# A decoder trunk with gated experts: router and gathered rows made from the unnormalised residual, and expert weights loaded in runs of four rows

## The chip, the cores and the metric

The kernel runs on one core of a Trainium2 chip. The time is the device time of one execution in microseconds (us); the median of three runs of the kernel before is 721.51 us (719.81 to 723.47).

## The reference

256 tokens of 1024 channels (float32) pass two layers. Each adds a mixer's output to the residual `h`, then that of a mixture of experts (MoE). The first mixer is an RWKV-7 recurrence, the second a stick-breaking attention. The MoE, where the change is made:

```python
def rmsnorm(x, g):
    return x * rsqrt(mean(x * x, -1) + 1e-6) * g

h = h + hier_moe(rmsnorm(h, norm_ffn[l]), ...)

def hier_moe(x, w_group, b_group, w_inner, b_inner, w_gate, w_up, w_down):
    pg = softmax(x @ w_group + b_group)          # 4 groups; the best one is taken
    pi = softmax(inner logits of that group)     # 4 experts of it; the best two are taken
    gates = p_group * renormalised top-2 weights # (tokens, 16 experts)
    h = silu(x @ w_gate[e]) * (x @ w_up[e]) * gates[:, e]    # 1024 -> 256
    return sum over e of h @ w_down[e]                       # 256 -> 1024
```

At the end the residual is normalised once more. Since the root factor of the norm is one number for a token, `x @ w` equals that number times `(h * g) @ w`.

## The kernel before

Phases run one after another: `rwkv`, `moe0`, `attn`, `moe1`. Each engine's program is written out by hand in the order in which it issues, and semaphores join them (`wait_ge`, `then_inc`); an engine that waits holds up all that stands behind it in its own program. The residual `h` lies token-major (two tiles `j` of 128 tokens by 1024 channels); a half `a` is 512 of the channels. The last projection of a mixer adds half 0 to `h` (DVE, L1164), and one weight piece (5.5 us) later half 1.

**Head of a MoE phase.** ACT squares `h` with a running sum (L702); DVE makes mean, reciprocal (L1136, L1137), ACT the root `rstd` (L706); DVE writes the normalised rows `xs` (L1171). TensorE waits with filler products of the identity matrix (`stay_warm`, L1738), turns `xs` into channel-major `xT` (L1747), ACT and DVE copy it from PSUM (L733, L1176); TensorE forms the logits in two steps (L2208, L2213) with ACT's copy `lgT` (L737) between. DVE adds the bias (`lg`, L1183), ranks (L1187 to L1192), marks `chosen` (L1218); TensorE counts places (L2221); DVE builds a 0/1 matrix `pick` (L1262) for each pair of experts with 64 slots for each expert. Meanwhile `xs` is split in two parts of lower precision whose sum is exact enough: `xt_hi` by ACT (L728), `xt_lo` by GpSimd (POOL, L672). TensorE gathers rows by a product of `pick` with both (L2244) and turns them (L2288), and the experts begin.

**Experts.** Eight pairs. For each: gate and up products in one row of PSUM, two experts side by side in column halves of the array (L2299), silu on ACT (L786), gate factor on DVE (L1289), down product (L2313), scattering back (L2329) and addition to `h` (L1303). 24 loads of 2 MB (two experts, half of gate and up, or the down weights) come through SyncE's queue in a ring of seven buffers (`load_bufs`, L458, L464); the two rings of the mixers' weights (`w_ring`) are two of them. In `moe0` the first two pieces of the attention's weights are split into high and low parts (ACT L691, DVE L1126) ahead of the last pair's silu in ACT's and DVE's programs.

## Time and profile before

| | |
|---|---|
| profiled execution, its span | 724.1 us, 721.9 us |
| granted TensorE clock, mean | 0.974 |
| TensorE busy (products) | 658.4 us, 91% |
| DVE / ACT / POOL busy | 354.8 / 272.5 / 101.7 us |
| read from memory | 143.11 MB |
| DMA packets under 2 KB, of all | 70449 of 97732 |

The page gives busy time for each engine, the span in 40 slices, the chain of work that ended last and the costliest groups. A timeline row names start, length, engine, line, what is written from what, and in brackets how long the engine stood idle before and what released it. The MoE phases cover about 275 to 424 and 563 to 714 us.

### The profile page before, as it was taken

How to read it: one execution, taken by the hardware profiler on the slowest of the kernel's cores; microseconds unless marked ns; L12 is line 12 of the kernel's file. 1: busy time of each engine (PE TensorE's matmuls, PEld its weight loads, DVE VectorE, ACT ScalarE, POOL GpSimd, SP SyncE). 2: the span in 40 equal slices, each digit the busy share in tenths (PEclk: the TensorE clock that was granted, in tenths of full speed). 3: DMA queues.
4: the chain of work that ended last, by engine and by line, in shares of the span. 5: the costliest groups of instructions: out<-in, count | busy, mean ns of one | idle time of the engine just before them, and what ended most of it. 6: DMA issues, size and time to landing. Idle time of an engine off the chain costs nothing. (4 is left out here: it accounts for less than half of the span.)

```text
span 721.9 us, 14225 instructions
## 1 busy us (share of the span) xinstructions
PE 658.4 (91%) x6183; PEld 455.1 (63%) x6183; DVE 354.8 (49%) x541; ACT 272.5 (38%) x387; POOL 101.7 (14%) x126
## 2 busy tenths in 40 slices
PE   2699989988988799999999999999979999999994
PEld 1575857868778578644444369997757864444442
DVE  3893896733565664312222455577734431222225
ACT  3454552442252513432222345566632342222213
POOL 9820054040032012000000000022210200000000
PEclk9799989999999999999999999999989999999999
DMA  9950532300000169999999821553104999999941
GB/s 260 301 188 14 182 131 111 96 4 5 4 4 5 60 208 364 369 365 367 366 366 377 301 94 60 175 156 136 60 0 132 357 366 367 367 367 368 367 165 60
DMA packets 97732, 145.15 MB, mean 201 GB/s; under 512 B 4745, under 2 KB 70449, under 8 KB 97665
## 3 DMA queue, kind: packets, MB, share of 16 engines
q1 hardware_dynamic: 96848, 142.28, 58.1%
q0 software_dynamic: 816, 1.90, 1.2%
q8 instruction: 52, 0.85, 0.5%
q14 instruction: 16, 0.12, 0.1%
HBM read 143.11 MB, written 1.05 MB: 200 GB/s over the span
## 5 line engine op out<-in xcount | busy, mean ns | idle before, releaser
L1126 DVE TENSOR_TENSOR w_lo<-w_ring,w_hi 128x2048 fp32r<-128x2048 f32 x32 | 75.5, 2366 | 22.7 <-PE ps L1756 16.6
L2299 PE MATMUL ps<-load,xe 128*64 128x512 f32 x384 | 85.8, 596 | 0.0
L691 ACT ACTIVATE w_hi<-w_ring 128x2048 fp32r<-128x2048 f32 x32 | 61.0, 1912 | 63.1 <-PE ps L1756 45.8
L1754 PE MATMUL ps<-w_hi,xa_hi 128*128 128x512 f32 x128 | 54.5, 426 | 13.9 <-DVE xa_lo L1390 8.8
L1289 DVE SCALAR_TENSOR_TENSOR hact_s<-silu_s,slot_gates,ps 128x256 f32<-128x256 f32 x16 | 7.7, 479 | 107.6 <-issue 81.8
L2299 PEld LDWEIGHTS ps<-load,xe 128*64 128x64 f32 x384 | 26.3, 137 | 48.3 <-issue 47.5
L1755 PE MATMUL ps<-w_lo,xa_hi 128*128 128x512 f32 x128 | 53.1, 415 | 0.0
L1756 PE MATMUL ps<-w_hi,xa_lo 128*128 128x512 f32 x128 | 53.0, 414 | 0.0
L664 POOL TENSOR_TENSOR att<-att,causal 128x256 f32<-128x256 f32 x16 | 15.0, 954 | 244.2 <-ACT att L1063 244.2
L2313 PE MATMUL ps<-load,hs 128*64 128x512 f32 x192 | 43.3, 593 | 0.5 <-DVE y_lo L1295 0.5
L786 ACT ACTIVATE silu_s<-ps 128x256 f32<-128x256 f32 x16 | 6.1, 383 | 95.3 <-PE ps L2299 60.2
L1754 PEld LDWEIGHTS ps<-w_hi,xa_hi 128*128 128x128 f32 x128 | 25.8, 202 | 22.3 <-DVE xa_lo L1390 9.2
L1303 DVE TENSOR_TENSOR h<-ps,h 128x512 f32<-128x512 f32 x48 | 30.6, 683 | 13.9 <-PE ps L2329 13.9
L1738 PE MATMUL ps<-ident 128*128 128x128 f32 x260 | 33.4, 286 | 2.4 <-DVE h L1164 1.6
L1738 PEld LDWEIGHTS ps<-ident 128*128 128x128 f32 x260 | 31.4, 199 | 4.6 <-DVE h L1164 2.4
L764 ACT ACTIVATE xg<-ps 128x512 f32<-128x512 f32 x32 | 19.2, 600 | 36.4 <-PE ps L2244 36.4
L1754 PE MATMUL ps<-w_hi,xb_hi 128*128 128x512 f32 x64 | 26.9, 420 | 5.2 <-issue 5.2
L2313 PEld LDWEIGHTS ps<-load,hs 128*64 128x64 f32 x192 | 14.0, 137 | 27.3 <-issue 27.3
L797 ACT ACTIVATE y_hi<-ps 128x1024 fp32r<-128x1024 f32 x14 | 14.4, 1026 | 42.5 <-PE ps L2313 39.7
L1756 PEld LDWEIGHTS ps<-w_hi,xa_lo 128*128 128x128 f32 x128 | 25.6, 200 | 6.5
L1755 PEld LDWEIGHTS ps<-w_lo,xa_hi 128*128 128x128 f32 x128 | 25.7, 201 | 5.8
L2244 PE MATMUL ps<-xt_hi,pick 128*128 128x512 f32 x64 | 26.5, 413 | 2.9 <-DVE y_lo L1295 2.1
(346 smaller groups left out, 1402.2 us busy)
## 6 DMA issues: line engine op xcount, KB each, us to landing
load<-in_moe_w_gate_dram SPq DMA_DIRECT2D x48, 512.0 KB, 9.0
load<-in_moe_w_up_dram SPq DMA_DIRECT2D x48, 512.0 KB, 8.9
load<-in_moe_w_down_dram SPq DMA_DIRECT2D x48, 512.0 KB, 8.7
w_ring<-in_rw_w_rkv_dram SPq DMA_DIRECT2D x24, 512.0 KB, 6.0
w_ring<-in_moe_w_gate_dram SPq DMA_DIRECT2D x16, 512.0 KB, 10.0
w_ring<-in_moe_w_up_dram SPq DMA_DIRECT2D x16, 512.0 KB, 9.7
w_ring<-in_moe_w_down_dram SPq DMA_DIRECT2D x16, 512.0 KB, 8.5
w_ring<-in_w_kv_dram SPq DMA_DIRECT2D x16, 512.0 KB, 5.0
```

Source lines behind the costliest of these rows:

```text
L664: m = nc.gpsimd.tensor_tensor(a[:, hh], a[:, hh], causal[:, :].unsqueeze(1).broadcast_to([P, 2, P]), ALU.mult)
L691: nc.scalar.activation(whi[n % HI][:, :, :], w_ring[n % RING][:, :, :], ACT.Copy).then_inc(hi_ready, 1)
L764: nc.scalar.activation(xg[:, a * HALF:(a + 1) * HALF], PS[:, (0 if p else 2) + a, :], ACT.Copy).then_inc(s["rows_out"], 1)
L1126: nc.vector.tensor_tensor(wlo[n % LO][:, :, :], w_ring[n % RING][:, :, :], whi[n % HI][:, :, :].bitcast(f32), ALU.subtract).then_inc(lo_re ...
L1303: nc.vector.tensor_tensor(sl, PS[:, bank + a, :], sl, ALU.add).then_inc(s["added"], 1)
L1738: nc.tensor.matmul(PS[:, bank, 0:P], ident[:, :], ident[:, :], start=True, stop=True)
L1754: nc.tensor.matmul(dst, xh, wh, start=start, stop=False)
L1755: nc.tensor.matmul(dst, xh, wl, start=False, stop=False)
L1756: return nc.tensor.matmul(dst, xl, wh, start=False, stop=stop)
L2244: m = nc.tensor.matmul(PS[:, (0 if p else 2) + a, :], pick[p % 2][:, j, :], x_[:, j, a * HALF:(a + 1) * HALF], start=j + part == 0, stop=j ...
L2299: m = nc.tensor.matmul(PS[rows(c), 4, :], xe[:, b, rows(c)], w[c][:, i, :], start=b == 0, stop=b == NC - 1)
L2313: m = nc.tensor.matmul(PS[rows(c), a, :], hs[:, f, rows(c)], w[c][:, f, a, :], start=f == 0, stop=f == NF - 1)
```

## The change

- The router and the gathered rows are made from `h` itself. TensorE turns raw `h` (half 0 as soon as the mixer's last product is issued, half 1 for each token tile as it is added); the norm weights are multiplied into the router's weights `wr` once (GpSimd). The root `rstd` enters later, as a factor of each token: in `lg`, in silu's scale and in the gates. `gates` carries both (gate times root, and root) through the gather, 32 columns in place of 16.
- `xs` is `h` times the weights. Half 0 is written by DVE between the two residual additions (`first_rows`), half 1 by GpSimd; the splits and the squares go by halves too. The mean of squares needs one more addition.
- Filler products: 22 before the transposes go, 5, 5, 6 become 4, 2, 3 (the 8 stay).
- The gate and up weights come with four consecutive rows of a matrix for each partition (4 KB in one run), so a product reads its moving operand as two runs of 256 at a distance of 4 KB; `xs` is written in the matching order of channels, by reads at a step of four elements (`by_row`).
- The weights' row `ffn_row` is loaded ahead of the first expert load. Load buffer 2 lies over the mixer's operand `xa` now and `moe0` waits with it for the last piece (`piece_used`); `xa` and `xb` trade places in the attention and in `xt`.

ScalarE, from the first MoE's table load to the logits' copy. The program before:

```order
L699 ACT_TABLE_LOAD [waits router_loaded]
L702 ACTIVATE ps,ss<-h 128x1024 [waits h_added] x2
L706 ACTIVATE rstd<-rec 128x2 [waits norm_recip]
L728 ACTIVATE xt_hi<-xs 128x1024 [waits norm_scaled]
L733 ACTIVATE xT<-ps 128x512 [waits norm_turned] x2
L728 ACTIVATE xt_hi<-xs 128x1024 [waits norm_scaled]
L737 ACTIVATE lgT<-ps 128x256 [waits moe_lgT_psum]
```

and after:

```order
L766 ACT_TABLE_LOAD
L754 ACTIVATE ps,ss<-h 128x512 [waits h_added]
L754 ACTIVATE ps,ss<-h 128x512 [waits norm_squares,h_added]
L759 ACTIVATE xt_hi<-xs 128x512 [waits norm_scaled] x2
L763 ACTIVATE xT<-ps 128x512 [waits norm_turned]
L754 ACTIVATE ps,ss<-h 128x512 [waits norm_squares,h_added]
L763 ACTIVATE xT<-ps 128x512 [waits norm_turned]
L754 ACTIVATE ps,ss<-h 128x512 [waits norm_squares,h_added]
L776 ACTIVATE rstd<-rec 128x2 [waits norm_recip]
L778 ACTIVATE lgT<-ps 128x256 [waits moe_lgT_psum]
L759 ACTIVATE xt_hi<-xs 128x512 [waits moe_xs_late] x2
```

The root moved behind both copies of `xT` and stands directly ahead of `lgT`; the late half's `xt_hi` follows it.

VectorE at the same place, from the first residual addition, before:

```order
L1164 TENSOR_TENSOR h<-ps,h 128x512 [waits piece_used,rw_x_again]
L1164 TENSOR_TENSOR h<-ps,h 128x512
L1164 TENSOR_TENSOR h<-ps,h 128x512 [waits piece_used]
L1164 TENSOR_TENSOR h<-ps,h 128x512
L1136 TENSOR_SCALAR ms<-ss 128x2 [waits norm_squares]
L1137 RECIPROCAL rec<-ms 128x2 [waits dve_step]
L1171 SCALAR_TENSOR_TENSOR xs<-h,rstd,ffn_row 128x1024 [waits moe_ffn_row,norm_rstd]
L1171 SCALAR_TENSOR_TENSOR xs<-h,rstd,ffn_row 128x1024
L1176 COPY xT<-ps 128x512 [waits norm_turned] x2
L1183 TENSOR_TENSOR lg<-ps,br_73 128x40 [waits moe_logits]
L1187 TENSOR_TENSOR r_cmp<-lg 128x40x4 [waits dve_step]
L1188 TENSOR_TENSOR r_cmp<-lg 128x40x4
```

and after:

```order
L1215 TENSOR_TENSOR h<-ps,h 128x512 [waits piece_used,rw_x_again]
L1215 TENSOR_TENSOR h<-ps,h 128x512
L1222 TENSOR_TENSOR xs<-h,ffn_row 128x512 [waits h_added,moe_ffn_row]
L1222 TENSOR_TENSOR xs<-h,ffn_row 128x512
L1215 TENSOR_TENSOR h<-ps,h 128x512 [waits piece_used]
L1215 TENSOR_TENSOR h<-ps,h 128x512
L1229 COPY xT<-ps 128x512 [waits norm_turned] x2
L1236 TENSOR_TENSOR ms<-ss 128x2 [waits norm_squares]
L1237 TENSOR_SCALAR ms<-ms 128x2 [waits dve_step]
L1238 RECIPROCAL rec<-ms 128x2 [waits dve_step]
L1242 SCALAR_TENSOR_TENSOR lg<-ps,rstd,br_73 128x20 [waits moe_logits,norm_rstd]
L1242 SCALAR_TENSOR_TENSOR lg<-ps,rstd,br_73 128x20
L1248 TENSOR_TENSOR r_cmp<-lg 128x40x4 [waits dve_step]
L1249 TENSOR_TENSOR r_cmp<-lg 128x40x4
```

The rows of half 0 stand between the additions; the rest of the norm (`ms`, `rec`) stands behind the copies of `xT`, and its first row reads two operands.

GpSimd from the last rows of the recurrence to the attention, before:

```order
L641 TENSOR_TENSOR vb<-v_s,bonus 128x512 [waits rw_vb_used]
L646 TENSOR_TENSOR vb<-vb,lnb_row 128x512 [waits rw_late_loaded,rw_pool_step]
L672 TENSOR_TENSOR xt_lo<-xs,xt_hi 128x1024 [waits moe_xt_hi] x2
```

and after:

```order
L649 TENSOR_TENSOR vb<-v_s,bonus 128x512 [waits rw_vb_used]
L654 TENSOR_TENSOR vb<-vb,lnb_row 128x512 [waits rw_late_loaded,rw_pool_step]
L691 TENSOR_TENSOR wr_64<-wr_64,cols 128x256 [waits cols_ready,router_loaded]
L691 TENSOR_TENSOR wr_65<-wr_65,cols 128x256
L683 TENSOR_TENSOR xt_lo<-xs,xt_hi 128x512 [waits moe_xt_hi] x2
L697 TENSOR_TENSOR xs<-h,ffn_row 128x512 [waits h_added,moe_ffn_row]
L697 TENSOR_TENSOR xs<-h,ffn_row 128x512 [waits h_added]
L683 TENSOR_TENSOR xt_lo<-xs,xt_hi 128x512 [waits moe_xt_hi] x2
L672 TENSOR_TENSOR att_154<-att_154,causal 128x2x128 [waits attn_exp]
```

GpSimd makes the late rows `xs` between its two subtractions, and two products for the router's weights come first.

The diff, without the attention's exchange of names, the sizes of tiles, the branch for overfull experts and the new gate rows:

```diff
@@ -227,7 +227,7 @@
 load_bufs = [load_buf(0, (R0 + 80 * KB, R0 + 96 * KB)), load_buf(1, (R0 + 88 * KB, R0 + 104 * KB)),
-             load_buf(2, (R0 + 16 * KB, R0 + 24 * KB)), w_ring[0:2], w_ring[2:4],
+             load_buf(2, (R0, R0 + 8 * KB)), w_ring[0:2], w_ring[2:4],
@@ -405,6 +405,13 @@
     return expert_sems[q], n + k * EXPERT[q]
+def by_row(v, a):
+    return v[:, a * HALF:(a + 1) * HALF].rearrange("p (c i) -> p i c", i=4)
+def by_row_out(j, a):
+    return xs[:, j, a * HALF:(a + 1) * HALF].rearrange("p (i c) -> p i c", i=4)
@@ -442,32 +449,33 @@
                 sp.wait_ge(lo_ready, before - (2 if q == 3 else 0))
-            elif q != 1 and (k or q != 2):
+            elif q != 1:
                 sp.wait_ge(piece_used, before)
...
                 first_use(q)
+                if i == 0:
+                    sp.dma_start(ffn_row[:, :], norm_ffn[k].partition_broadcast(P)
+                                 ).then_inc(moe_sems["ffn_row"], 16)
             else:
...
                     for a, w in ((0, moe_w_gate), (1, moe_w_up)):
-                        sp.dma_start(dst[:, :, a * F:(a + 1) * F],
-                                     w[k, e, half * HALF:(half + 1) * HALF, :].rearrange("(b p) f -> p b f", p=P)
+                        rows = w[k, e, half * HALF:(half + 1) * HALF, :]
+                        sp.dma_start(dst[:, 2 * a:2 * a + 2, :],
+                                     rows.rearrange("(p q i) f -> p q (i f)", p=P, q=2)
                                      ).then_inc(load_in[q], 16)
...
                                      ).then_inc(load_in[q], 16)
-            if i == 1:
-                sp.dma_start(ffn_row[:, :], norm_ffn[k].partition_broadcast(P)
-                             ).then_inc(moe_sems["ffn_row"], 16)
-                if f"moe{k}" == PHASES[-1]:
-                    sp.dma_start(gain_row[:, :], norm_final.partition_broadcast(P)).then_inc(gain_loaded, 16)
+            if i == 1 and f"moe{k}" == PHASES[-1]:
+                sp.dma_start(gain_row[:, :], norm_final.partition_broadcast(P)).then_inc(gain_loaded, 16)
@@ -666,11 +674,29 @@
     def moe_phase(k):
-        s = moe_sems
+        s, nm = moe_sems, norms[f"moe{k}"]
+        def row_lo(a):
+            for j in range(NT):
+                pool.wait_ge(s["xt_hi"], k * PER["xt_hi"] + NT * a + j + 1)
+                sl = (slice(None), j, slice(a * HALF, (a + 1) * HALF))
+                nc.gpsimd.tensor_tensor(xt_lo[sl], xs[sl], xt_hi[sl].bitcast(f32), ALU.subtract
+                                        ).then_inc(s["xt_lo"], 1)
+        if k == 0:
+            pool.wait_ge(router_loaded, 16 * 8)
+            pool.wait_ge(cols_ready, 1)
+            for i in range(2):
+                gain = cols[:, 16 + NC * i:16 + NC * (i + 1)].unsqueeze(2).broadcast_to([P, NC, LT])
+                nc.gpsimd.tensor_tensor(wr[i][:, :, :], wr[i][:, :, :], gain, ALU.mult
+                                        ).then_inc(slots_ready, 1)
+        row_lo(0)
+        pool.wait_ge(s["ffn_row"], 16 * (k + 1))
         for j in range(NT):
-            pool.wait_ge(s["xt_hi"], k * PER["xt_hi"] + j + 1)
-            nc.gpsimd.tensor_tensor(xt_lo[:, j, :], xs[:, j, :], xt_hi[:, j, :].bitcast(f32), ALU.subtract
-                                    ).then_inc(s["xt_lo"], 1)
+            pool.wait_ge(nm.h_ready[0], nm.h_ready[1][j])
+            nc.gpsimd.tensor_tensor(by_row_out(j, 1), by_row(h[:, j, :], 1), by_row(ffn_row[:, :], 1), ALU.mult
+                                    ).then_inc(s["xs_late"], 1)
+        row_lo(1)
@@ -720,21 +746,39 @@
         s, nm = moe_sems, norms[f"moe{k}"]
-        if k == 0:
-            act.wait_ge(router_loaded, 16 * 8)
-        norm_stats(nm)
-        def row_hi(j):
-            act.wait_ge(*nm.at("scaled", j + 1))
-            nc.scalar.activation(xt_hi[:, j, :], xs[:, j, :], ACT.Copy).then_inc(s["xt_hi"], 1)
-        row_hi(0)
-        for i in range(2):
+        def square(j, a):
+            act.wait_ge(nm.h_ready[0], nm.h_ready[1][0] - NT + NT * a + j)
+            if a + j:
+                act.wait_ge(*nm.at("squares", NT * a + j))
+            nc.scalar.activation(PS[:, 2, :], h[:, j, a * HALF:(a + 1) * HALF], ACT.Square,
+                                 accum_out=ss[:, NT * a + j:NT * a + j + 1]).then_inc(norm_sems["squares"], 1)
+        def row_hi(j, a):
+            sl = (slice(None), j, slice(a * HALF, (a + 1) * HALF))
+            nc.scalar.activation(xt_hi[sl], xs[sl], ACT.Copy).then_inc(s["xt_hi"], 1)
+        def turned(i):
             act.wait_ge(*nm.at("turned", i + 1))
...
                                  ACT.Copy).then_inc(s["xT_act"], 1)
-        row_hi(1)
+        act.preload_act_table(ACT.Sqrt)
+        for j in range(NT):
+            square(j, 0)
+        for j in range(NT):
+            act.wait_ge(*nm.at("scaled", j + 1))
+            row_hi(j, 0)
+        for i in range(2):
+            turned(i)
+            square(i, 1)
+        act.wait_ge(*nm.at("recip", 1))
+        nc.scalar.activation(rstd[:, :], rec[:, :], ACT.Sqrt).then_inc(norm_sems["rstd"], 1)
         act.wait_ge(s["lgT_psum"], k * PER["lgT_psum"] + 1)
         nc.scalar.activation(lgT[:, :], PS[:, 0, 0:T], ACT.Copy).then_inc(s["lgT"], 1)
+        for j in range(NT):
+            act.wait_ge(s["xs_late"], k * PER["xs_late"] + j + 1)
+            row_hi(j, 1)
@@ -781,9 +825,11 @@
             act.wait_ge(load_used, k * NL + load_no("in", p, 1) + 1)
+            act.wait_ge(s["gates_out"], p + 1)
             if p:
                 act.wait_ge(*ex(k, "hact", 4 * p))
-            nc.scalar.activation(silu_s[:, :], PS[:, 4, 0:F], ACT.Silu).then_inc(expert_sems["silu"], 4)
+            nc.scalar.activation(silu_s[:, :], PS[:, 4, 0:F], ACT.Silu, scale=slot_gates[p % 2][:, 1:2]
+                                 ).then_inc(expert_sems["silu"], 4)
@@ -1163,14 +1214,16 @@
+    def first_rows(k):
+        dve.wait_ge(moe_sems["ffn_row"], 16 * (k + 1))
+        dve.wait_ge(norms[f"moe{k}"].h_ready[0], norms[f"moe{k}"].h_ready[1][0] - 1)
+        for j in range(NT):
+            nc.vector.tensor_tensor(by_row_out(j, 0), by_row(h[:, j, :], 0), by_row(ffn_row[:, :], 0), ALU.mult
+                                    ).then_inc(norm_sems["scaled"], 1)
     def moe_phase(k):
         s, nm = moe_sems, norms[f"moe{k}"]
-        norm_rstd(nm)
-        dve.wait_ge(s["ffn_row"], 16 * (k + 1))
-        for j in range(NT):
-            nc.vector.scalar_tensor_tensor(out=xs[:, j, :], in0=h[:, j, :], scalar=rstd[:, j:j + 1],
-                                           in1=ffn_row[:, :], op0=ALU.mult, op1=ALU.mult
-                                           ).then_inc(norm_sems["scaled"], 1)
@@ -1179,9 +1232,17 @@
         other, own = sets.unsqueeze(2).broadcast_to([P, NS, EG, EG]), sets.unsqueeze(3).broadcast_to([P, NS, EG, EG])
+        dve.wait_ge(*nm.at("squares", 2 * NT))
+        link(nc.vector.tensor_tensor(ms[:, :], ss[:, 0:NT], ss[:, NT:2 * NT], ALU.add))
+        link(nc.vector.tensor_scalar(ms[:, :], ms[:, :], 1.0 / C, RMS_EPS, ALU.mult, ALU.add))
+        nc.vector.reciprocal(rec[:, :], ms[:, :]).then_inc(norm_sems["recip"], 1)
+        dve.wait_ge(*nm.at("rstd", 1))
         dve.wait_ge(s["logits"], k * PER["logits"] + 1)
-        link(nc.vector.tensor_tensor(lg[:, :, :], PS[:, 0, 0:NT * NR].rearrange("p (j r) -> p j r", j=NT),
-                                     br[k][:, :].unsqueeze(1).broadcast_to([P, NT, NR]), ALU.add))
+        for j in range(NT):
+            m = nc.vector.scalar_tensor_tensor(out=lg[:, j, :], in0=PS[:, 0, j * NR:(j + 1) * NR],
+                                               scalar=rstd[:, j:j + 1], in1=br[k][:, :], op0=ALU.mult,
+                                               op1=ALU.add)
+        link(m)
@@ -1624,6 +1687,7 @@
         split_next(14)
+        first_rows(0)
@@ -2199,15 +2265,23 @@
         s, nm = moe_sems, norms[f"moe{k}"]
-        norm(nm)
-        stay_warm(5, 3)
+        for a in range(2):
+            for j in range(NT):
+                pe.wait_ge(nm.h_ready[0], nm.h_ready[1][j] if a else nm.h_ready[1][0] - 1)
+                for b in range(4 * a, 4 * a + 4):
+                    m = nc.tensor.transpose(PS[:, 4 + b // 2, (b % 2) * T + j * P:(b % 2) * T + (j + 1) * P],
+                                            h[:, j, b * P:(b + 1) * P], ident[:, :])
+                    if j == NT - 1 and b % 2:
+                        m.then_inc(norm_sems["turned"], 1)
+        stay_warm(4, 3)
+        pe.wait_ge(slots_ready, 8)
         for b in range(NC):
...
         m.then_inc(s["lgT_psum"], 1)
-        stay_warm(5, 3)
+        stay_warm(2, 3)
@@ -2221,8 +2295,7 @@
         m.then_inc(s["places"], 1)
-        stay_warm(6, 3)
-        pe.wait_ge(s["xt_lo"], k * PER["xt_lo"] + NT)
+        stay_warm(3, 3)
@@ -2239,6 +2312,8 @@
         for a in range(2):
+            if p == 0:
+                pe.wait_ge(moe_sems["xt_lo"], k * PER["xt_lo"] + NT * (a + 1))
@@ -2250,6 +2325,10 @@
         return load_bufs[i % BUFS]
+    def by_rows(t):
+        return t[:, :, :].rearrange("p (a q) (i f) -> p (q i) a f", a=2, i=2)
@@ -2292,11 +2371,12 @@
             pe.wait_ge(s["x_out"], 2 * p + half + 1)
-            w = loaded(k, load_no("in", p, half))
+            w = [by_rows(t) for t in loaded(k, load_no("in", p, half))]
             for i in range(4):
...
                 for c in range(2):
-                    m = nc.tensor.matmul(PS[rows(c), 4, :], xe[:, b, rows(c)], w[c][:, i, :],
+                    m = nc.tensor.matmul(PS[rows(c), 4, :].rearrange("p (a f) -> p a f", a=2),
+                                         xe[:, b, rows(c)], w[c][:, i, :, :],
```

## Rows read from the trace of the kernel before

**Rows 1.** Chain that ended last, in order of time, second MoE: start us, us, what

```profile
661.08 7.02 PE ps L2299 x32
668.09 3.43 PE ps L2313 x16
...
677.28 7.02 PE ps L2299 x32
```

**Rows 2.** Timeline, VectorE, head of first MoE: start, us, engine line, out<-in, idle before

```profile
269.43 1.29 DVE L1164 TENSOR_TENSOR h<-ps,h 128x512 f32<-128x512 f32 x2 [3.94 <-PE ps L1756]
274.96 1.29 DVE L1164 TENSOR_TENSOR h<-ps,h 128x512 f32<-128x512 f32 x2 [4.24 <-PE ps L1756]
277.91 0.17 DVE L1136 TENSOR_SCALAR ms<-ss 128x2 f32<-128x2 f32 x1 [1.66 <-ACT ps L702]
...
282.45 1.29 DVE L1176 COPY xT<-ps 128x512 f32<-128x512 f32 x2 [1.42 <-PE ps L1747]
286.46 0.20 DVE L1183 TENSOR_TENSOR lg<-ps,br 128x40 f32<-128x40 f32 x1 [2.71 <-PE ps L2213]
286.69 0.32 DVE L1187 TENSOR_TENSOR r_cmp<-lg 128x160 f32<-128x160 f32 x1
...
289.84 0.42 DVE L1262 TENSOR_TENSOR pick<-slot_no,place_in 128x256 fp32r<-128x256 f32 x1
```

**Rows 3.** Timeline, ScalarE, the same stretch

```profile
275.69 1.03 ACT L702 ACTIVATE ps<-h 128x1024 f32<-128x1024 f32 x1 [11.81 <-DVE h L1164]
...
282.02 1.09 ACT L733 ACTIVATE xT<-ps 128x512 f32<-128x512 f32 x2 [1.09 <-PE ps L1747]
...
284.82 0.38 ACT L737 ACTIVATE lgT<-ps 128x256 f32<-128x256 f32 x1 [0.77 <-PE ps L2208]
```

**Rows 4.** Timeline, TensorE, the same stretch

```profile
280.73 1.91 PE L1747 MATMUL ps<-ident,xs 128*128 128x128 f32 x16
...
285.90 0.52 PE L2213 MATMUL ps<-add_tiles,lgT 128*128 128x20 f32 x4
286.27 2.03 PE L1738 MATMUL ps<-ident 128*128 128x128 f32 x16
...
290.77 0.48 PE L2244 MATMUL ps<-xt_hi,pick 128*128 128x512 f32 x1
...
294.30 3.65 PE L2299 MATMUL ps<-load,xe 128*64 128x512 f32 x16
```

**Rows 5.** Timeline, TensorE, first gathered rows of the second MoE

```profile
579.32 0.48 PE L2244 MATMUL ps<-xt_hi,pick 128*128 128x512 f32 x1
```

**Rows 6.** Timeline, GpSimd and VectorE, rwkv phase and first MoE

```profile
91.97 5.42 POOL L617 TENSOR_TENSOR yb<-r_tok,k_s 128x512 f32<-128x512 f32 x2 [50.46 <-DVE k_s L1451]
...
92.99 3.25 DVE L1126 TENSOR_TENSOR w_lo<-w_ring,w_hi 128x2048 fp32r<-128x2048 f32 x1
...
281.01 2.37 POOL L672 TENSOR_TENSOR xt_lo<-xs,xt_hi 128x1024 fp32r<-128x1024 f32 x1 [24.77 <-ACT xt_hi L728]
```

**Rows 7.** Line 617 on GpSimd, four products: ns min/median/max, first and last start

```profile
L617 POOL TENSOR_TENSOR yb<-r_tok,k_s x4: 2112/2202/3337, 92.0 to 119.6; 128x512 f32<-128x512 f32 x4
```

**Rows 8.** Timeline of TensorE, then a 1 us window: busy per engine, PEclk, DMA, GB/s

```profile
434.42 0.39 PE L1754 MATMUL ps<-xa_hi,w_hi 128*128 128x256 f32 x1 [1.97 <-DVE xa_lo L1152]
...
435.00:436.00 1.00, 1.00 (x8) 1.00 (x7) 1.00 (x4) 1.00 (x4) 0.00 (x0) 0.63 0.00 0
```

**Rows 9.** Windows, last two columns DMA share and GB/s

```profile
294.00:296.00 2.00, 2.00 (x12) 0.85 (x12) 0.00 (x0) 1.75 (x2) 0.00 (x0) 1.00 1.10 348
...
392.00:396.00 4.00, 4.00 (x21) 1.30 (x19) 0.00 (x0) 0.17 (x1) 0.00 (x0) 1.00 1.03 410
...
408.00:412.00 4.00, 4.00 (x22) 1.33 (x20) 2.29 (x2) 3.75 (x3) 0.00 (x0) 1.00 0.47 176
```

**Rows 10.** Timelines of ScalarE and of SyncE's queue, end of the first MoE

```profile
407.77 3.71 ACT L691 ACTIVATE w_hi<-w_ring 128x2048 fp32r<-128x2048 f32 x2 [6.21 <-PE ps L2299]
411.38 0.36 ACT L786 ACTIVATE silu_s<-ps 128x256 f32<-128x256 f32 x1
...
392.39 3.20 SPq L63 DMA_DIRECT2D w_ring<-in_w_kv_dram  x4
```

More of the change, by code:

```diff
@@ L200, in trunk_program @@
         r_s = mplace("r_s", [P, 10, NT])
-        slot_gates = [mplace(f"slot_gates{i}", [P, 1]) for i in range(2)]
+        slot_gates = [mplace(f"slot_gates{i}", [P, 2]) for i in range(2)]
         xg_at = off[0]
@@ L354, in __init__ @@
                 s.before = dict(norm_counts)
[L355 removed]
+                for q, n in (("squares", NT * halves), ("recip", 1), ("rstd", 1), ("scaled", NT),
                              ("turned", 4 * turned), ("hi", 4 * len(gains)), ("lo", 4 * len(gains))):
@@ L364, in trunk_program @@
         norms = {}
-        PER = dict(xT_act=2, xT_dve=2, lgT_psum=1, lgT=1, logits=1, gate_args=2, gate_exps=2, chosen=1, places=1, n_max=1, gates=1,
-                   xt_hi=NT, xt_lo=NT, gates_parts=1, ffn_row=16)
+        PER = dict(xT_act=2, xT_dve=2, lgT_psum=1, lgT=1, logits=1, gate_args=2, gate_exps=2, chosen=1, places=1, n_max=1,
+                   xs_late=NT, xt_hi=2 * NT, xt_lo=2 * NT, gates_parts=1, ffn_row=16)
         moe_sems = {q: sem(f"moe_{q}") for q in PER}
@@ L826, in all_experts @@
             def all_experts(k):
+                s = packed_sems[k]
+                act.wait_ge(s["x_psum"], 3)
+                for i in range(2):
+                    nc.scalar.activation(xT[:, 4 * i:4 * i + 4, :].rearrange("p (n b) t -> p n (b t)", n=2),
+                                         PS[:, 4 + 2 * i:6 + 2 * i, :], ACT.Copy).then_inc(s["x_out"], 1)
                 gate_exps(k)
@@ L2201, in moe_phase @@
                 s, nm = moe_sems, norms[f"moe{k}"]
-                norm(nm)
-                stay_warm(5, 3)
+                for a in range(2):
+                    for j in range(NT):
[7 more added lines that the diff above has]
+                pe.wait_ge(slots_ready, 8)
                 for b in range(NC):
@@ L2403, in all_experts @@
                     for half in range(2):
-                        w = loaded(k, load_no("in", p, half))
+                        w = [by_rows(t) for t in loaded(k, load_no("in", p, half))]
                         for c in range(2):
```

73 lines of the change are left out of this document (42 added, 31 removed).

## Prediction

> **What bounds the kernel now.** I read the chain of waits first. In the expert part of a MoE phase it stays on TensorE: one pair's gate and up products 7.02 us, the down products 3.43, the next pair 16.2 after the last [rows 1], with nothing but products between. An expert's row saved elsewhere is worth nothing there. Then I read the timelines of the three engines at the head of the first MoE, as one chain: second residual addition at 274.96, squares 275.69, mean 277.91, logits' bias 286.46, first `pick` 289.84, gathered rows 290.77, first expert product 294.30 [rows 2 to 4]. So 15.81 us pass from the addition to the gather, in which TensorE runs filler. The second MoE gathers at 579.32 [rows 5], the same distance behind its own addition. All of the change's worth is there, twice. Last I read the DMA windows: the expert loads keep the queues full, at 348 GB/s while only gate and up weights move and at 410 while down weights and mixer pieces do [rows 9].
>
> **The head, step by step.** Times count from the second addition (274.96 = 0).
> - Two additions of 0.65, so token tile 0 is ready at 0.65 and tile 1 at 1.3 (1.29 for two [rows 2]). Sixteen transposes take 1.91, 0.12 each [rows 4]: half 0's eight run from 0 to 1.0, half 1's fours end at 1.5 and 1.9.
> - VectorE copies two banks in 1.29 [rows 2]: from 1.8 to 3.1. ScalarE, in its new order: copy, square, copy, square. A copy of 512 is 0.55 (1.09 for two), a square of 1024 1.03 plus the sum's read [rows 3]; half of it with that read is about 0.65. From 0.75 that makes 3.15.
> - Mean on VectorE, three small instructions of 0.17 (0.2 apart) where there were two: 3.75. Root: 4.0.
> - The router needs the last copy (3.1) and ends at about 4.0, beside the root. `lgT` 0.38 [rows 3] to 4.4. From the second logit product to `lg` 0.56 (285.90 to 286.46 [rows 2, 4]): `lg` at 5.0.
>
> Before, `lg` stood at 286.46 - 274.96 = 11.5, so 6.5 us are gained. Two bias instructions in place of one add 0.1. From `lg` to the end of `pick` 3.8 stay (286.46 to 290.26 [rows 2]); the gather began 0.51 behind `pick`, behind fillers, and with three fillers fewer (16 instruction rows of filler are 2.03 us [rows 4], so six rows are 0.75) it begins at once: +0.45. Sum without any new wait: gather at 5.0 + 0.1 + 3.8 + 0.05 = 8.95, 6.9 us earlier.
>
> **New waits, which the sum must pay.**
> - *GpSimd beside VectorE.* In the trace, when both work on two SBUF operands, they take turns by whole instructions: two GpSimd products took 5.42 and VectorE's split of 2048, which takes 2.28 elsewhere, took 3.25 beside them [rows 6]. Before, GpSimd's last subtraction ended just as `lg` began. Now the late `xt_hi` follows `lgT` on ScalarE, GpSimd subtracts half rows of 1.19 (half of 2.37 [rows 6]) from 5.0 to 6.2 and again, and VectorE's rank comparisons (two operands in SBUF) begin at 5.35. The first waits 0.85, the second 1.2 behind the other subtraction. Bounds: 0 (VectorE is always served first) and 2.4 (both subtractions whole). I take 2.05. Who waits behind: ranks, `chosen`, places, `pick`, the gather.
> - *TensorE's clock.* The eight fillers behind the logits last 2.03 [rows 4], to about 7.05; `chosen` comes at 5.35 + 2.1 + 2.05 = 9.5. That is 2.4 us of idleness. After 1.97 idle at 434.42 the granted clock fell in the window at 435 to 0.63, towards the lower level of 1.2 GHz [rows 8]. The eight gather products (0.23 apart) and the turns would then take up to 1.9 longer. Bounds 0 and 1.9; I take 0.9.
> - *Strided reads.* The rows of half 0 on VectorE (two, 0.65 each if a step of four costs nothing) have from 270.7 to 274.96: 4.2 us of cover, so they may cost three times that and still nothing. The late rows on GpSimd have no row with such a step; the nearest are 1.19 as above and 2.2 in the median for line 617, in turns with VectorE [rows 7]. At 1.19 both end at 3.1, just ahead of the mean: 0. At 2.2 they end at 5.15 and the mean, whose first row now reads two SBUF operands, waits 2.0. I take 0, the uncontended row.
>
> The Trainium skill speaks against this step: in "Vector Engine (DVE) Microarchitecture Reference", section 5.2, reads that hop at every element cost 1.7 to 2.5 ns for a column in place of 1.05. No row here shows it. By it, estimated, half 0 would take up to 2.7 us, still under cover, and only if GpSimd paid the same would the head lose what the third rival loses.
>
> Per phase 6.9 - 2.05 - 0.9 = 3.9 us, twice 7.8.
>
> **What is added at nothing.** The router's weights times the norm weights: two GpSimd products of 256 columns, about 0.6 each by rows 6, at 256 to 258, beside VectorE's last splits; these may slip 1.2, TensorE has 2 us of older pieces to do, and the SyncE queue's first expert load waits for `z_tok` and slips too, with 24 us to its use. Gates: two more small instructions (0.4) inside a chain that ended 1.6 us before its use. Silu waits for `gates_out`, done three us before. Gather of 32 columns: those products are paced by the weight load. `ffn_row` first in the queue: 0.5 MB, 1.4 us for loads that lie 20 us ahead.
>
> **Loads.** Load 2 now waits for 274.96. Loads 0 and 1 and the row, 4.7 MB, are through by 272, so the queue stands still some 5 us. What can be late is the end of the first MoE: ScalarE splits two mixer pieces (407.77, 3.71 for both) ahead of silu (411.38), which stood behind them for 0.2 at most; SyncE issued the first at 392.39, when its buffer came free, and the queues ran dry in 408 to 412 [rows 9, 10]. With packets of 4 KB I take the 410 of [rows 9] for all loads: 22 loads of 2.1 MB from 277 end by 390, pieces are limited by their buffers and land by 395, and the gain stays. The Trainium skill, "DMA: Bandwidth & Descriptors", section Specifications, gives about 358 GB/s as the memory's limit for a core; by that, longer packets would bring next to nothing. The trace does not agree: 410 with longer packets [rows 9].
>
> **Sum.** Profiled span 721.9 - 7.8 = 714.1, its execution 724.1 - 7.8 = 716.3. That execution lies 2.6 above the median of 721.5, so in the median of runs 713.7.
>
> **Rivals.**
> 1. *No turns lost.* VectorE's small instructions slip in ahead of GpSimd and the clock stays at 2.4 GHz: 2 x 6.9 = 13.8, 707.7. For it: the operands are short. Against: rows 6 show strict turns.
> 2. *The queue holds the first MoE's end.* If gate and up weights still come at 348 GB/s, 14 of those 22 loads need 84 us and the rest 41: 402, the two pieces 408; the splits on ScalarE and VectorE then run to 413 and the last pair's gate factor is only 1.5 us earlier than now. Gain 3.9 + 1.5 = 5.4: 716.1. For it: the idle 5 us. Against: 410 in rows 9.
> 3. *Slow late rows.* GpSimd at 2.2 for each [rows 7]: 6.9 - 2.0 - 2.05 - 1.9 = 0.9 for a phase, 719.7, within the noise.
> 4. *Slower: the gate and up products read two runs.* No row shows a moving operand with a jump of 4 KB inside. 32 products take 7.02 us, and there are 16 such groups. From 7% (0.49 us for a group) the gain is gone; at 14% it is 713.7 + 15.7 = 729.4. For it: nothing in the trace; against: a jump once in 256 columns.
>
> **How the numbers follow.** Forecast 0.5, rival 1 0.2, rival 2 0.1, rival 3 0.12, rival 4 0.05, others 0.03. The forecast's own costs have the ends 0 and 4.3 a phase, which gives 707.7 to 718.9; with rival 3 the range of 8 in 10 is 707.5 to 719. A difference under 0.5% (3.6 us) can't be told from none: faster means below 717.9. Forecast, rival 1 and rival 2 lie there but for their upper tail: 0.8. Same 0.14, slower 0.06.
>
> **What would show it.** Raw transposes right behind the mixer's last product; `lg` 5 us after the second addition, not 11.5; the first comparison or the second lasting over a microsecond beside a GpSimd subtraction; PEclk at 0.5 to 0.7 near the gather or not; gather 10.5 to 11.5 us after the addition; GpSimd's late rows at 1.2 or at 2.2; windows of expert loads at 400 GB/s and pauses in them; groups of 32 gate and up products at 7.02. I am wrong if those groups lengthen, if `ms` stands waiting, or if ScalarE's last silu of the first MoE comes no earlier.

## The result and the profile after

The change makes the kernel a little faster: the changed kernel's median is 717.96 us (711.33 to 721.77, 19 runs), that of the kernel before 722.42 us (718.79 to 724.72, 19 runs). The ratio is 0.9941, with a 95% interval of 0.9920 to 0.9962: a gain of 4.3 us, between 2.7 and 5.8. Forecast was a gain of 7.8. In the profiled execution (718.0 us) the span is 716.2 us against 721.9, at a mean granted clock of 0.968 against 0.974.

VectorE at the head of the first MoE after the change; the second residual addition begins at 274.10:

```profile
274.10 1.29 DVE L1215 TENSOR_TENSOR h<-ps,h 128x512 f32<-128x512 f32 x2 [2.06 <-PE ps L1822]
275.93 1.29 DVE L1229 COPY xT<-ps 128x512 f32<-128x512 f32 x2 [0.54 <-PE ps L2272]
277.13 2.02 DVE L1236 TENSOR_TENSOR ms<-ss 128x2 f32<-128x2 f32 x1
...
280.85 0.39 DVE L1242 SCALAR_TENSOR_TENSOR lg<-ps,rstd,br 128x20 f32<-128x20 f32 x2 [1.30 <-PE ps L2287]
281.28 0.83 DVE L1248 TENSOR_TENSOR r_cmp<-lg 128x160 f32<-128x160 f32 x1
282.03 1.39 DVE L1249 TENSOR_TENSOR r_cmp<-lg 128x160 f32<-128x160 f32 x1
...
286.01 0.42 DVE L1324 TENSOR_TENSOR pick<-slot_no,place_in 128x256 fp32r<-128x256 f32 x1
```

GpSimd in the same stretch:

```profile
271.79 2.66 POOL L683 TENSOR_TENSOR xt_lo<-xs,xt_hi 128x512 fp32r<-128x512 f32 x2 [15.00 <-ACT xt_hi L759]
274.94 4.20 POOL L697 TENSOR_TENSOR xs<-h,ffn_row 128x512 f32<-128x512 f32 x2 [0.49 <-DVE h L1215]
280.66 2.58 POOL L683 TENSOR_TENSOR xt_lo<-xs,xt_hi 128x512 fp32r<-128x512 f32 x2 [1.52 <-ACT xt_hi L759]
```

Read the two together. The `ms` addition of two columns, 0.15 of work, lasts 2.02 us and ends at 279.15, as GpSimd's second late row does at 279.14. The two comparisons, 0.32 each before [rows 2], last 0.83 and 1.39 beside the late subtractions. `lg` comes 6.75 us after the addition, where it was 11.5. That `ms` stands waiting is one of the signs that the prediction named for its being wrong.

TensorE at the head of the second MoE, addition at 559.67:

```profile
566.15 2.03 PE L1804 MATMUL ps<-ident 128*128 128x128 f32 x16
570.58 0.28 PE L2295 MATMUL ps<-chosen,causal_r 128*128 128x16 f32 x1 [2.40 <-DVE chosen L1279]
...
571.33 1.63 PE L1804 MATMUL ps<-ident 128*128 128x128 f32 x6
572.61 0.77 PE L2319 MATMUL ps<-xt_hi,pick 128*128 128x512 f32 x1
573.19 0.63 PE L2319 MATMUL ps<-xt_lo,pick 128*128 128x512 f32 x1
...
577.00 3.65 PE L2378 MATMUL ps<-load,xe 128*64 128x512 f32 x16
```

After 2.40 us in which TensorE is idle, six filler rows take 1.63 in place of 0.91 and a gather product 0.63 in place of 0.39. The window there, and two with expert loads (columns as in [rows 8, 9]):

```profile
571.00:572.00 1.00, 1.00 (x6) 1.00 (x6) 0.45 (x2) 0.00 (x0) 0.00 (x0) 0.50 1.04 414
...
304.00:308.00 4.00, 4.00 (x22) 1.33 (x20) 0.00 (x0) 0.42 (x2) 0.00 (x0) 1.00 1.03 412
...
404.00:408.00 4.00, 4.00 (x22) 1.30 (x20) 2.32 (x2) 3.81 (x3) 0.00 (x0) 1.00 0.00 0
```

The clock is at 0.50, its lower level, in the first. The loads run at 412 GB/s where [rows 9] had 348, and from 404 to 408 the queue is empty, while [rows 9] had 176 still in 408 to 412. The last silu of the first MoE went with it:

```profile
403.73 3.71 ACT L717 ACTIVATE w_hi<-w_ring 128x2048 fp32r<-128x2048 f32 x2 [6.21 <-PE ps L2378]
407.35 0.46 ACT L831 ACTIVATE silu_s<-ps,slot_gates 128x256 f32<-128x256 f32 x1
```

That silu is 133.25 us after the addition; it was 136.42 in the kernel before [rows 2, 10]. Groups of 32 gate and up products take 7.09 us at that end in both kernels.

From the addition to the first expert product the first MoE needs 15.97 us (290.07 - 274.10) where it needed 19.34, the second 17.33 where it needed 19.35 (582.86 - 563.51 in the trace of before). Heads: 3.37 + 2.02 = 5.4 us. The second addition of the first MoE, from which all this is counted, itself comes 0.86 us earlier, behind a recurrence where stretches of low clock differ between executions. Behind the first MoE 0.54 is lost: the attention's fillers begin 2.75 us after VectorE's last additions to `h` begin (L1394 at 419.25), where it was 2.21.

```profile
419.25 2.48 DVE L1394 TENSOR_TENSOR h<-ps,h 128x512 f32<-128x512 f32 x4 [1.18 <-PE ps L2409]
422.00 5.18 PE L1804 MATMUL ps<-ident 128*128 128x128 f32 x44 [1.38 <-DVE h L1394]
```

### The profile page after: what moved, and what is told of

Its sections match the earlier page's. It is cut to its first block and busy times, and to the rows that moved or that the text cites. A ratio compares the mean times of both kernels' runs of the same rounds, so it can differ in the third digit from the quotient of the medians.

```text
span 716.2 us, 14050 instructions
## 1 busy us (share of the span) xinstructions
PE 649.0 (91%) x6067; PEld 445.0 (62%) x6067; DVE 362.7 (51%) x549; ACT 275.1 (38%) x399; POOL 113.9 (16%) x136
## 3 DMA queue, kind: packets, MB, share of 16 engines
HBM read 143.11 MB, written 1.05 MB: 201 GB/s over the span
## 5 line engine op out<-in xcount | busy, mean ns | idle before, releaser
L831 ACT ACTIVATE silu_s<-ps,slot_gates 128x256 f32<-128x256 f32 x16 | 7.6, 472 | 95.4 <-PE ps L2378 69.9
L2378 PE MATMUL ps<-w_ring,xe 128*64 128x512 f32 x128 | 28.7, 595 | 0.0
L2409 PE MATMUL ps<-y_hi,pick_t 128*128 128x512 f32 x64 | 26.6, 416 | 2.1 <-DVE h L1365 2.1
```

Of the source, the lines that this page charges most:

```text
L2378: m = nc.tensor.matmul(PS[rows(c), 4, :].rearrange("p (a f) -> p a f", a=2), xe[:, b, rows(c)], w[c][:, i, :, :], start=b == 0, stop=b == ...
L2409: m = nc.tensor.matmul(PS[:, bank, :], pick_t[p % 4][:, j * P:(j + 1) * P], y_[:, a, :], start=first and part == 0, stop=last and part == 1)
```

## Experiments

The columns `lg`, gather and first expert give the start of the first such instruction in each run's own profile, in us after the second addition; `lg` is the same in both phases within 0.02. "First expert" is the first gate and up product.

| kernel | median us | ratio to before (95%) | `lg` | gather, first / second MoE | first expert |
|---|---|---|---|---|---|
| changed | 717.96 | 0.9941 (0.9920 to 0.9962) | 6.75 | 12.39 / 12.94 | 15.97 / 17.33 |
| plain_rows | 718.53 | 0.9938 (0.9907 to 0.9968) | 5.14 | 10.79 / 10.76 | 15.69 / 15.55 |
| ms_scalar | 715.39 | 0.9913 (0.9879 to 0.9947) | 6.57 | 12.21 / 12.60 | 15.78 / 17.12 |
| sub_vector | 713.52 | 0.9860 (0.9824 to 0.9897) | 6.77 | 11.36 / 10.83 | 14.94 / 14.41 |
| more_fill | 720.54 | 0.9974 (0.9956 to 0.9992) | 6.75 | 12.39 / 12.38 | 15.96 / 15.96 |
| row_split | 712.67 | 0.9871 (0.9843 to 0.9898) | 5.14 | 10.92 / 10.27 | 15.20 / 13.85 |
| both | 709.94 | 0.9831 (0.9797 to 0.9865) | 5.14 | 9.18 / 9.18 | 12.77 / 12.77 |
| ms_columns | 713.98 | 0.9882 (0.9854 to 0.9911) | 5.15 | 11.72 / 10.80 | 16.93 / 15.68 |
| wide_fill | 715.29 | 0.9906 (0.9874 to 0.9938) | 6.75 | 13.06 / 12.39 | 16.64 / 15.97 |
| both_plain | 714.69 | 0.9902 (0.9868 to 0.9937) | 5.14 | 9.18 / 9.19 | 12.77 / 12.75 |

The rows of the heads repeat from kernel to kernel to a few hundredths; the times do not. In ms_scalar each head is only 0.2 us shorter than in the changed kernel, yet its ratio from six runs is 0.0028 lower, 2 us. The second addition of the first MoE stands anywhere between 271.29 and 276.74 us in the eleven profiles. So a difference of some 2 us between two edited kernels is not settled by their medians. The times missed what was expected for the theory that the rows bear out by 3.7 us in plain_rows (718.53 for 714.8, or 1.5 for the 717 of late loads), by 3.0 in more_fill (720.54 for 717.5 at most), by 2.3 in row_split (712.67 for 715 at least) and by 1.0 in ms_columns.

### Without the runs of four rows (plain_rows)

```diff
-return v[:, a * HALF:(a + 1) * HALF].rearrange("p (c i) -> p i c", i=4)
+return v[:, a * HALF:(a + 1) * HALF]
-sp.dma_start(dst[:, 2 * a:2 * a + 2, :], rows.rearrange("(p q i) f -> p q (i f)", p=P, q=2)
+sp.dma_start(dst[:, :, a * F:(a + 1) * F], rows.rearrange("(b p) f -> p b f", p=P)
```

The products that read these buffers are changed to match; those lines are left out here.

> The changed kernel without its runs of four rows: weights come in rows of 1 KB again, and GpSimd's late rows read and write every element in turn. Changed kernel: late rows 2.10 us each, ms stands 1.85 us behind the second one, gather 12.4 us behind the second addition. Theory A (the step of four costs GpSimd the time): late rows at 1.3 like its subtractions, both over by 3.4 us after the addition, ms waits 0.4, gather at 10.8; 3.2 us faster over two phases if the loads at 348 to 364 GB/s do not hold the end of the first MoE (714.8), 717 if they do. Theory B (GpSimd is slow there because VectorE copies beside it): late rows stay at 2.1, gather stays at 12.4, time 718 or up to 2 us more from the slower loads.

VectorE and GpSimd (addition at 272.31), then ScalarE and TensorE at the end of the first MoE:

```profile
275.34 0.34 DVE L1235 TENSOR_TENSOR ms<-ss 128x2 f32<-128x2 f32 x1
```

```profile
273.15 2.52 POOL L696 TENSOR_TENSOR xs<-h,ffn_row 128x512 f32<-128x512 f32 x2 [0.95 <-DVE h L1214]
```

```profile
403.93 1.91 ACT L716 ACTIVATE w_hi<-w_ring 128x2048 fp32r<-128x2048 f32 x1 [8.48 <-DMA w_ring<-in_w_kv_dram]
406.64 1.91 ACT L716 ACTIVATE w_hi<-w_ring 128x2048 fp32r<-128x2048 f32 x1 [0.81 <-DMA w_ring<-in_w_kv_dram]
408.46 0.46 ACT L830 ACTIVATE silu_s<-ps,slot_gates 128x256 f32<-128x256 f32 x1
```

```profile
411.33 0.44 PE L2402 MATMUL ps<-ident,hact_s 128*128 128x128 f32 x2 [2.94 <-DVE hact_s L1350]
```

Theory A: a late row takes 1.26 us in place of 2.10 with the same copies beside it, so the step of four costs GpSimd the time, and `ms` waits 0.2. Theory B is out. `lg` gains 1.6 us in each head. The clock fell in both gathers (eight products from 10.79 to 14.24 in the first, 3.4 us where the changed kernel needs 2.1), so the first head keeps only 0.3 of it; in the second, where the clock fell in the changed kernel too, the first expert product comes 1.8 us earlier. But at the end of the first MoE ScalarE waits for mixer pieces that land late, with silu behind them; TensorE stands 2.94 us, and the clock falls there too. The attention's fillers begin 151.3 us after the addition; with the runs it is 147.9.

### The sum of squares by one-tensor instructions (ms_scalar), then by single columns (ms_columns)

```diff
-link(nc.vector.tensor_tensor(ms[:, :], ss[:, 0:NT], ss[:, NT:2 * NT], ALU.add))
+for j in range(NT):
+    m = nc.vector.tensor_scalar(ms[:, j:j + 1], ss[:, j:j + 1], ss[:, NT + j:NT + j + 1], None, ALU.add)
+link(m)
```

> The changed kernel, with the sum of the two halves' squares made by two instructions of VectorE that read one tensor and take the second half as a per-partition scalar, in place of one that reads two tensors. Theory A (only instructions with two tensors in SBUF are held by a GpSimd instruction that runs): they slip through beside the late rows, rec at 3.7 us after the addition in place of 5.5, gather at 10.6, 3.5 us faster in all: 714.5. Theory B (every VectorE instruction with its operand in SBUF is held): ms still stands till GpSimd's second late row ends, gather at 12.5, time 718.2. Theory C (ms waited for ScalarE's squares, not for GpSimd): no change either, and ms starts no earlier.

```profile
274.31 0.33 DVE L1237 TENSOR_SCALAR ms<-ss 128x1 f32<-128x1 f32 x2
274.67 1.69 DVE L1239 TENSOR_SCALAR ms<-ms 128x2 f32<-128x2 f32 x1
```

Neither theory holds. Two instructions on one column pass beside GpSimd's row; the next, one tensor and two constants but two columns wide, is held until the row ends. Theory C is out: the squares were there at 3.0. The Trainium skill has the rule ("SBUF — State Buffer", section "Who interferes with whom"): an instruction with one source is kept waiting by GpSimd only where it runs in a mode that takes both read ports, one with two sources in SBUF wherever GpSimd reads there too. By the Trainium skill that mode takes outermost dimensions longer than one that are both even, or equal, in source and result ("VectorE: DVE Perf Modes", section "What auto-detection actually checks"). What the engine does with a single column, which has no such dimension, that section does not say; that it stays out of the mode is my reading. So the second run splits all three steps into single columns (the scaling and the reciprocal in loops over `j` like the one above):

> The changed kernel with the mean and its reciprocal worked out one column at a time (six instructions of 128 by 1 where there were three of 128 by 2). In the run before, two instructions on one column began and ended beside GpSimd's late row (0.33 for both) and the next, on two columns, stood 1.69 till it ended. Theory A (an instruction on a single column is never held, its width is what counts): rec at 3.9, lg at 5.2, gather at 10.9, up to 3 us less and half of that lost to the clock: 715 to 716.5. Theory B (the first two got through by chance or because they were on their way already): one of the later ones is held till 5.05 all the same, gather at 12.3, 718.

```profile
276.06 0.21 DVE L1240 TENSOR_SCALAR ms<-ms 128x1 f32<-128x1 f32 x2
276.31 0.23 DVE L1243 RECIPROCAL rec<-ms 128x1 f32<-128x1 f32 x2
```

```profile
273.51 4.20 POOL L697 TENSOR_TENSOR xs<-h,ffn_row 128x512 f32<-128x512 f32 x2 [0.49 <-DVE h L1215]
```

Theory A holds: six instructions pass within 0.84 us while GpSimd's rows run on to 277.7, and `lg` comes 1.6 us earlier. Part of it goes to the clock again: TensorE stands 2.44 us ahead of `chosen` and the first MoE's first expert product is later than in the changed kernel (16.93).

### The late subtractions on VectorE (sub_vector)

```diff
 nc.vector.reciprocal(rec[:, :], ms[:, :]).then_inc(norm_sems["recip"], 1)
+late_lo(k, 0)        # xt_lo of the second half, token tile 0
 ...
 m.then_inc(s["chosen"], 1)
+late_lo(k, 1)
-row_lo(1)            # in GpSimd's program
```

ScalarE's copy `xt_hi` of token tile 0 moves ahead of the root too, so that VectorE finds it.

> The changed kernel, with the two late subtractions (xt_lo, second half) moved from GpSimd to VectorE: the first behind rec, where VectorE stands idle 1.3 us, the second behind chosen, where it stands idle 0.8. GpSimd has nothing beside the rank comparisons then. Theory A (they take turns): r_cmp 0.32 each again in place of 0.83 and 1.39, pick 1.6 us earlier, gather at 10.7, and TensorE idle 1.6 less before chosen, so that its clock stays at 2.4 GHz in the second phase (0.8 more): 718 - 3.2 - 0.8 = 714. Theory B (the comparisons are slow of themselves, by their broadcast operands): they stay at 0.8 and 1.4, and nothing is gained: 718.

```profile
283.93 0.32 DVE L1257 TENSOR_TENSOR r_cmp<-lg 128x160 f32<-128x160 f32 x1
284.17 0.32 DVE L1258 TENSOR_TENSOR r_cmp<-lg 128x160 f32<-128x160 f32 x1
```

Theory A holds: 0.32 each again, so their broadcast operands are not what was slow. `chosen` comes 1.6 us earlier, TensorE's idle time ahead of it in the second MoE is 0.82 in place of 2.40, and the gather there runs at full clock. In the first MoE the clock falls behind 1.50 us of idle time ahead of the logits, and the slowed fillers run on past `chosen`: the gather begins at 11.36 there, 10.83 in the second.

### More filler behind the logits: more instructions (more_fill), wider ones (wide_fill)

```diff
-stay_warm(2, 3) ... stay_warm(8, 3)      # ahead of and behind the logits
+stay_warm(8, 3) ... stay_warm(18, 3)     # more_fill
+stay_warm(2, 3) ... eight products of identity and h[:, 0, 0:256]     # wide_fill
```

> The changed kernel with 18 filler products in place of 8 behind the logits and 8 in place of 2 ahead of them, so that TensorE has no idle stretch over 0.5 us between its transposes and chosen. Theory A (the idle 2.4 us there drop the clock and this costs): the gather of the second MoE keeps 0.39 for a product, its first expert product comes 0.8 to 1 us earlier; in all 716.5 to 717.5. Theory B (the clock costs nothing on the chain, or falls for another reason): 718, and if the fillers run over, up to 1 us more.

```profile
420.97 0.40 PE L2409 MATMUL ps<-y_lo,pick_t 128*128 128x512 f32 x1
425.61 6.37 PE L1804 MATMUL ps<-ident 128*128 128x128 f32 x44 [4.24 <-issue]
```

The head did what theory A says: 15.96 in both phases, 1.4 less. But the kernel is not faster than the changed one. Its loss stands at the end of the first MoE, where TensorE leaves the experts' branch (`pe.If`): 4.24 us idle, released by nothing that the profile names ("issue"), and half clock behind it. In the changed kernel it is 1.38, and the profile names VectorE's last addition; counted from the start of those additions the fillers begin 5.61 us later here, 2.75 there. The fillers of the attention begin 150.75 us after the addition, 2.85 later than in the changed kernel. Sixteen more filler products in each head are the only difference; why they should bring the wait is open. So the next run adds columns and no instruction:

> The changed kernel; the eight filler products behind the logits have 256 columns in place of 128, so that TensorE is busy to within 0.5 us of chosen with not one instruction more. Theory A (idle time there drops the clock; what the run with more fillers lost, it lost at the end of the first MoE where TensorE stood 4.24 us for instructions): first expert product at 15.96 in both phases, 1.4 us less, no stall at that end: 716.6. Theory B (more filling costs clock elsewhere): over 718.5 again, with more half-clock stretches in the rest of the trace.

In the second MoE theory A holds: idle 0.73, 15.97, and the wait at that end is 1.01. In the first the clock had fallen behind the 1.47 us of idleness ahead of the logits; the wide fillers took 5.39 us in place of 3.70 and held TensorE until after `chosen` (16.64). The ratios (0.9906, changed kernel 0.9941) have intervals that overlap: what the clock costs is read from the rows, not settled by the times. Nor does one profile without the long wait show that the number of instructions makes it.

### The second late row on VectorE (row_split)

```diff
-for j in range(NT):                     # GpSimd
-    ... by_row_out(j, 1), by_row(h[:, j, :], 1)
+    ... by_row_out(0, 1), by_row(h[:, 0, :], 1)
+nc.vector.tensor_tensor(by_row_out(1, 1), by_row(h[:, 1, :], 1), by_row(ffn_row[:, :], 1), ALU.mult)   # behind rec
```

Here too ScalarE's `xt_hi` of token tile 0 moves ahead of the root.

> The changed kernel with the second of the two late rows moved from GpSimd to VectorE, behind rec, where it stands idle 1.3 us for the root and the logits; GpSimd's one late row is over 2.95 us after the addition, when ms wants to begin (3.03). The first late subtraction can start earlier. Theory A (ms is held by the late rows): ms starts and ends at once, rec at 3.7 in place of 5.5; what GpSimd then subtracts beside the comparisons still costs up to 1.8; gather at 10.6 to 11.2, and TensorE, idle as long as before, loses its clock there in some heads: 715 to 717. Theory B (the chain is bound by ScalarE and TensorE ahead of lg, VectorE's wait hides behind them): lg stays at 6.75, 718.

```profile
273.83 2.13 POOL L696 TENSOR_TENSOR xs<-h,ffn_row 128x512 f32<-128x512 f32 x1 [0.48 <-DVE h L1215]
276.03 0.15 DVE L1236 TENSOR_TENSOR ms<-ss 128x2 f32<-128x2 f32 x1
278.82 1.38 DVE L1251 TENSOR_TENSOR r_cmp<-lg 128x160 f32<-128x160 f32 x1
```

`ms` begins behind GpSimd's one late row and lasts 0.15, and `lg` stands at 5.14: theory A. The second comparison is still held by a subtraction (1.38); the first, ahead of it, is not (0.34).

### GpSimd off the chain (both)

The edits of row_split, and both late subtractions on VectorE, behind `chosen` and behind `n_max`.

> The second late row on VectorE behind rec, and both late subtractions on VectorE too (behind chosen, and behind n_max): GpSimd works beside nothing on the chain. If the waits on GpSimd are the whole of what the forecast sum missed and the two add up: lg at 5.1 after the addition, r_cmp 0.32 each, pick at 8.7, gather at 9.2, first expert product at 12.8 in both phases where the changed kernel has 15.97 and 17.33: 7.7 less, 710.3. If the loads or the clock take it back: 713.5, no better than with the subtractions moved alone.

VectorE (addition at 272.72), then TensorE:

```profile
275.75 0.15 DVE L1243 TENSOR_TENSOR ms<-ss 128x2 f32<-128x2 f32 x1
...
276.21 1.08 DVE L1246 TENSOR_TENSOR xs<-h,ffn_row 128x512 f32<-128x512 f32 x1
277.86 0.38 DVE L1251 SCALAR_TENSOR_TENSOR lg<-ps,rstd,br 128x20 f32<-128x20 f32 x2 [0.57 <-PE ps L2298]
278.27 0.32 DVE L1257 TENSOR_TENSOR r_cmp<-lg 128x160 f32<-128x160 f32 x1
278.52 0.32 DVE L1258 TENSOR_TENSOR r_cmp<-lg 128x160 f32<-128x160 f32 x1
```

```profile
280.43 0.28 PE L2306 MATMUL ps<-chosen,causal_r 128*128 128x16 f32 x1 [0.82 <-DVE chosen L1290]
```

Every landmark came within 0.1 us of what was written, in both phases. That the median came within 0.4 is in part luck: three of the six runs lie at 707.1 to 708.0 and three at 711.9 to 712.7, and the median falls between. This version beats both kernels: 1.7% below before (1.35% to 2.03%), some 8 us below the changed one. In both heads the clock holds: TensorE has no idle stretch ahead of the logits (1.47 in the changed kernel) and 0.82 ahead of `chosen`, because the chain that got shorter is the one it was waiting for.

### The same, without the runs (both_plain)

> The kernel with GpSimd off the chain (second late row and late subtractions on VectorE), without the runs of four rows: gate and up weights in rows of 1 KB. Theory A (the queue, full from the second addition on, sets the end of the first MoE: in the run without the runs TensorE stood 2.94 us there for the last gate factor, behind weight pieces that landed late): the earlier head of the first MoE is worth nothing, its last silu stays 136 us behind the addition and the attention's fillers 151.3; only the second MoE keeps its 2.8 us: 715.7, 5.8 more than with the runs. Theory B (the loads follow the buffers that experts give back, so they come earlier with the head): last silu at 133, 712.5.

```profile
413.05 0.69 PE L2413 MATMUL ps<-ident,hact_s 128*128 128x128 f32 x2 [5.79 <-DVE hact_s L1361]
```

Theory A holds: the last silu stands at 136.1 after the addition as in plain_rows, though the head is 2.9 us shorter; TensorE waits 5.79 where it waited 2.94. The attention's fillers begin 151.3 us after the addition, 144.2 with the runs. So without the runs the queue of loads sets the end of the first MoE at either length of head, and with them the shorter head keeps its worth there: 0.9831 with them, 0.9902 without.

One thing that this leaves open is a cost of the change itself: load 2 now waits for the last piece, and the queue runs low until the second addition. The window from 272 to 276, before and then plain_rows:

```profile
272.00:276.00 4.00, 3.22 (x15) 2.32 (x14) 1.03 (x2) 0.31 (x1) 0.00 (x0) 1.00 1.06 364
272.00:276.00 4.00, 4.00 (x42) 3.09 (x40) 3.09 (x7) 2.30 (x6) 2.71 (x3) 1.00 0.61 187
```

With 268 to 272 (349 and 295 GB/s) that is 0.9 MB less, an estimated 2.6 us of loading at 350 GB/s. A kernel without the runs that keeps load 2 early was not run, so how much of the runs' worth only pays this pause back is not shown.

## Why the prediction was off

**The way was right, the size was not.** The gain is 4.3 us, forecast 7.8. The chain that was followed (addition, transposes, copies, mean, root, logits, ranks, pick, gather) is the chain that moved, by 5.4 us of 7.8 in the profiled heads.

**The step that failed is "Strided reads": GpSimd's late rows at 1.19, cost 0.** They take 2.10 each with a step of four, 1.26 without (plain_rows). By the forecast's own 2.2 end the mean waits 2.0; measured, `lg` stands at 6.75, and at 5.14 in every version whose `ms` is not held: 1.6 a phase, 3.2 in all. I took the uncontended, unstrided row, though VectorE's strided rows had cover for three times their price and GpSimd's had none: without cover the upper end is the one to take. The Trainium skill's rule in "Vector Engine (DVE) Microarchitecture Reference", section 5.2 (reads that hop cost 1.7 to 2.5 ns for a column in place of 1.05), held on VectorE: 512 columns take 1.08 us there and 0.67 without the step (both, both_plain), 2.1 ns for a column in place of 1.3 with the instruction's fixed part in both. A page of the Trainium skill that I had not weighed speaks of programs written for GpSimd's own processors: in "GPSIMD Engine Reference", section "Performance pitfalls for Q7 kernels", a read step over 8 bytes costs some 50% more for an element. The step here is 16 bytes, and the runs show 67% for this built-in product. The third rival named this wait, but with all other costs at their upper ends (719.7).

**A slip in the range.** With the forecast's own costs at their upper end, 4.3 a phase, 2.6 a phase are left, twice 5.2: 716.3 us. The text took off one phase only and has 718.9. By the right sum the measured 717.96 and the gain of 4.3 lie outside what the forecast's own costs allow, because the wait on the late rows was not among them; that they still lie in the stated range is no merit of the forecast.

**Turns on the comparisons: 2.05 forecast, 1.6 measured.** From `lg` to `pick` 5.16 us in the changed kernel, 3.56 in "both", where GpSimd does nothing beside them. The first rival (no turns lost) is out.

**The clock: 0.9 a phase forecast, 0 and 1.4 measured.** From the first places product to the first expert product: 5.05 us in the first MoE, 6.42 in the second, 5.06 in both heads of "both". In the first MoE the lower clock fell on fillers, which nobody waits for; in plain_rows, row_split and ms_columns it hit the first MoE's gather. The same 1.9 us of idle time ahead of `chosen` in both heads of row_split brought the lower clock in the first and not in the second, so the price of a head does not follow from that idle time alone; it ran from 0 to 1.4 us in these kernels and to 2.5 in the first head of ms_columns.

**`lg` without waits: 5.0 forecast, 5.14 measured.** So the working of the head was sound, but for what runs beside it.

**Sum.** Two heads: 2 x 1.6 lost on `ms`, 2 x 0.14 on the rest of the way to `lg`, 2 x 0.45 won on the turns, 0.4 won on the clock make 2.2 of the 2.4 us by which the profiled heads (5.4) miss 7.8. Another 0.54 went behind the first MoE, where TensorE leaves the experts' branch; the forecast had no term for it. The median's gain, 4.3, agrees with what is left within its interval.

**Loads.** 410 GB/s forecast, 404 to 413 measured in the windows of 4 us from 288 to 372. The Trainium skill's figure of some 358 ("DMA: Bandwidth & Descriptors", section Specifications) is exceeded by these windows once more; the row divides a memory's bandwidth by two cores, and here one core runs. The second rival (the queue holds the first MoE's end) did not happen here, but plain_rows and both_plain show that it would have at the old rate: the attention's fillers begin 3.4 us later than in the changed kernel, and 7.05 later than in "both". With it stands a term that the forecast put at nothing, the pause of the queue before load 2: measured with the runs on, it cost no wait. The fourth rival (products that read two runs) is out: 7.09 us before and after. At nothing, as said: the new products on `wr` (they stretched two of VectorE's instructions at 255 to 257 from 0.69 to 0.99 each, and TensorE had older pieces to do), the gates, the wider gather of gates.

## What to carry to other kernels

A GpSimd instruction on SBUF operands beside a chain of tiny VectorE instructions costs the chain up to the whole GpSimd instruction, unless the tiny ones work on one column at a time; its length matters, not theirs. So price moved work on the engine that it lands on with the access pattern that it will have there, and ask which small instruction comes due while it runs. Shortening a head is worth only as much as the next constraint leaves (here the load queue at the first MoE's end): bring both or measure both. An idle gap of TensorE is paid twice when the clock falls behind it; in "both" the shorter chain was also the one that kept the clock in the heads. And work a range's ends out for as many phases as the forecast.
